# Two decoder layers on one core: the layer loop written out, page numbers read before the wait, and a new order of units in the down projections

## The reference, cut to what matters

```python
def swiglu(x, wg, wu, wd):
    return (jax.nn.silu(x @ wg) * (x @ wu)) @ wd        # D_MODEL 1024, D_FF 2816

def trunk_layer(h, ...):
    h = h + 0.5 * swiglu(rmsnorm(h, norm_ffn1), ffn1_gate, ffn1_up, ffn1_down)
    x = rmsnorm(h, norm_mix)
    z = x @ w_in + b_in            # split into the four mixers' columns and four gates
    # conformer convolution, retention, gated linear attention, differential attention
    merged = einsum(branches, w_branch, sigmoid(gates))
    h = h + merged @ w_out
    h = h + 0.5 * swiglu(rmsnorm(h, norm_ffn2), ffn2_gate, ffn2_up, ffn2_down)
```

## Time and profile before

| what | value |
|---|---|
| median of three executions | 2910.8 us |
| the profiled execution, its own time | 2914.48 us |
| its span, first to last instruction | 2912.9 us |
| PE busy | 2866.3 us, 98% |
| DVE busy | 2040.4 us, 70% |
| ACT busy | 1230.1 us, 42% |
| POOL busy | 121.1 us, 4% |
| DMA | 321.00 MB, 110 GB/s |
| a page of keys, request to landing, median | 2.9 us |
| a page of values, the same | 3.2 us |

### The profile page before, as it was taken

How to read it: one execution, slowest core, us unless ns; L and a number is a source line. 1 busy time by engine, 2 the same in 40 slices (tenths; PEclk the granted TensorE clock), 3 DMA queues, 4 the chain that set the end, 5 groups by cost and what they waited for, 6 DMA issues and landing times.

```text
span 2912.9 us, 59977 instructions
## 1 busy us (share of the span) xinstructions
PE 2866.3 (98%) x21668; PEld 2743.9 (94%) x21668; DVE 2040.4 (70%) x3643; ACT 1230.1 (42%) x2192; POOL 121.1 (4%) x219
## 2 busy tenths in 40 slices
PE   8999999999999999999999999999999999999998
PEld 7999999988889999999999999998878899999998
DVE  8889434567657688886488893346666576888854
ACT  6446223435325254454254452243352343544632
POOL 0000001220000000000000000012100000000000
PEclk9999999999999999999999999999999999999999
DMA  4223225562324312223222222436423243122232
GB/s 143 91 86 105 99 82 181 172 198 77 109 70 157 137 61 88 99 87 112 77 74 87 101 103 93 138 126 206 159 72 109 86 161 121 61 101 86 101 102 91
DMA packets 102131, 321.00 MB, mean 110 GB/s; under 512 B 13503, under 2 KB 30063, under 8 KB 100272
## 3 DMA queue, kind: packets, MB, share of 16 engines
q1 hardware_dynamic: 89424, 277.03, 27.3%
q0 software_dynamic: 12512, 41.43, 4.4%
HBM read 290.62 MB, written 29.12 MB: 110 GB/s over the span
## 4 chain that ended last, share of the span: by engine, by line
PE 90%; DVE 4%; issue 3%; POOLq 1%; ACT 1%; DMA 0%; POOL 0%; DVEq 0%; SPq 0%; ACTq 0%
PE ps L1304 46%; PE ps L1333 34%; PE ps L1483 3%; PE ps L1316 2%; PE ps L1749 1%; PE ps L1545 1%; POOLq L615 1%; DVE Z L2321 1%; DVE w_lo L1875 1%; PE ps L1621 0%; POOL vpage L616 0%; PE ps L1595 0%; PE ps L1771 0%; PE ps L1645 0%; PE ps L1644 0%
## 5 line engine op out<-in xcount | busy, mean ns | idle before, releaser
L1875 DVE TENSOR_TENSOR w_lo<-w_raw,w_hi 128x1024 fp32r<-128x1024 f32 x240 | 292.5, 1223 | 369.1 <-ACT w_hi L727 366.1
L1333 PE MATMUL ps<-x_more,w_hi 128*128 128x296 f32 x2112 | 460.3, 299 | 2.1 <-DVE p_copy L2028 1.4
L1333 PE MATMUL ps<-x_hi,w_hi 128*128 128x296 f32 x1408 | 421.6, 299 | 3.4 <-DVE hT L2146 2.1
L1333 PE MATMUL ps<-x_hi,w_lo 128*128 128x296 f32 x1408 | 422.2, 300 | 0.0
L1333 PE MATMUL ps<-x_lo,w_hi 128*128 128x296 f32 x1408 | 422.1, 300 | 0.0
L727 ACT ACTIVATE w_hi<-w_raw 128x1024 fp32r<-128x1024 f32 x224 | 234.7, 1053 | 396.7 <-PE ps L1304 198.8
L1304 PE MATMUL ps<-x_hi,w_hi 128*128 128x296 f32 x1600 | 371.7, 314 | 1.8 <-ACT hT L1054 1.6
L1913 DVE TENSOR_TENSOR w_lo<-w_raw,w_hi 128x512 fp32r<-128x512 f32 x444 | 299.5, 689 | 96.6 <-ACT w_hi L775 96.3
L1333 PEld LDWEIGHTS ps<-x_more,w_hi 128*128 128x128 f32 x2112 | 351.2, 188 | 4.3 <-DVE p_copy L2028 2.4
L1304 PE MATMUL ps<-x_lo,w_hi 128*128 128x296 f32 x1600 | 350.3, 300 | 0.0
L1304 PE MATMUL ps<-x_hi,w_lo 128*128 128x296 f32 x1600 | 349.8, 300 | 0.0
(11 more groups left out here) (367 smaller groups left out, 5089.5 us busy)
## 6 DMA issues: line engine op xcount, KB each, us to landing
w_raw<-wstream SPq DMA_DIRECT2D x420, 512.0 KB, 3.5
kpage<-cache_k SPq DMA_DIRECT2D x128, 128.0 KB, 2.9
vpage<-cache_v POOLq DMA_DIRECT2D x128, 128.0 KB, 3.2
gate_rows<-hT SPq DMA_DIRECT2D x48, 296.0 KB, 2.5
d_sg<-gate_rows SPq DMA_DIRECT2D x16, 888.0 KB, 4.7
h_rows<-hT SPq DMA_DIRECT2D x2, 1480.0 KB, 6.2
hT<-h_rows SPq DMA_DIRECT2D x2, 1480.0 KB, 6.3
hT<-h_in SPq DMA_DIRECT2D x4, 592.0 KB, 8.1
```

The lines of the kernel that those rows point to most:

```text
L1333: mm = pe.matmul(ps[:, bank, 0:HALF], wp[:, k, :], xp, start=new and k == 0 and n == 0, stop=k == KH - 1 and n == 2, skip_group_check=True)
L1875: v.tensor_tensor(w_lo[:, slot, :, :], w_raw[:, slot, :, :], w_hi[:, slot, :, :].bitcast(F32), ALU.subtract).then_inc(weights_low, 1)
```

## The change

Five edits:

1. On all five engines `Fori(0, DEPTH)` becomes a Python loop: the instructions of both layers stand one after the other and l is a constant. The shorter loops inside stay.
2. POOL's `load_values` takes the page numbers from `page_numbers`, which reads all 16 of a pass into registers; for passes 1 to 3 this stands ahead of the wait on `sample_pv`.
3. In the down projections PE takes the units in the order DOWN_ORDER: tile 0's unit 0, tile 1's unit 0, tile 0's units 1 and 2, tile 1's units 1 and 2, then tiles 2 and 3 as before; the same for tiles 4 to 7. `units_multiplied` is counted so that it keeps to the order of the stream: nothing at tile 1's unit 0, two at tile 0's unit 2.
4. OUT_PAIRS becomes (1, 2, 0, 3): tiles 1 and 5 go to pair 2, tiles 2 and 6 to pair 0. The waits of `begin` and of S1 in the next feed-forward stage are exchanged to fit; tile 1 and tile 2 of the down projection wait for DVE's quarters that read the banks.
5. At the end of a feed-forward stage the orders of DVE and ACT change, as below.

```diff
-OUT_PAIRS = (1, 0, 2, 3)
+OUT_PAIRS = (1, 2, 0, 3)
+DOWN_ORDER = ((0, 0), (1, 0), (0, 1), (0, 2), (1, 1), (1, 2)) + tuple((j, u) for j in (2, 3) for u in range(3))
...
-            def load_values(l, p):
-                for b in (2 * p, 2 * p + 1):
-                    for pg in range(PAGES):
-                        page = pl.value_load(pages[0:1, b * PAGES + pg:b * PAGES + pg + 1], min_val=0, max_val=POOL - 1)
-                        pl.dma_start(vpage[:, b % 2, pg, :], cache_v[ds(l * POOL + page, 1)]...).then_inc(values_loaded[b % 2], 16)
+            def page_numbers(p):
+                return [pl.value_load(pages[0:1, n:n + 1], min_val=0, max_val=POOL - 1) for n in range(2 * p * PAGES, 2 * (p + 1) * PAGES)]
+            def load_values(l, numbers):
+                for n, page in enumerate(numbers):
+                    b2, pg = divmod(n, PAGES)
+                    pl.dma_start(vpage[:, b2, pg, :], cache_v[ds(l * POOL + page, 1)]...).then_inc(values_loaded[b2], 16)
...
+                numbers = page_numbers(1)
                 pl.wait_ge(sample_pv, 1)
-                load_values(l, 1)
+                load_values(l, numbers)
...
 # ACT, last pair (after out_unit(2))
-                tanh(N0 + KF - 1)
                 hidden_tiles(6, 8)
                 act.wait_ge(products_done, last + 7)
-                hidden_tiles(8, 12)
                 out_unit(3)
-                hidden_tiles(12, KF)
+                hidden_tiles(8, 10)
+                tanh(N0 + KF - 1)
+                hidden_tiles(10, KF)
...
-            with act.Fori(0, DEPTH) as l:        # the same on pe, v, pl and sp
+            for l in range(DEPTH):
...
 # PE
-                pe.wait_ge(residual_added, l * 24 + 8 + 10 if f else l * 24 + 2)
+                pe.wait_ge(residual_added, l * 24 + 8 + 11 if f else l * 24 + 3)
                 begin(N0, 0)
...
+                    for j, u in DOWN_ORDER:
+                        pos = j * 3 + u
+                        unit_ready(l * QUADS + first // RING + i * 3 + pos // RING, pos % RING)
+                        if u == 0:
+                            pe.wait_ge(residual_added, l * 24 + r0 + i * 4 + j + 1)
+                        if (j, u) == (1, 0):
+                            pe.wait_ge(pair_steps, PAIR_STEPS * (hidden + KF - 1 + 2) + 3)
+                        elif (j, u) == (2, 0):
+                            pe.wait_ge(pair_steps, PAIR_STEPS * (hidden + KF - 1 + 2) + 6)
...
+                        if (j, u) == (0, 2):
+                            last.then_inc(units_multiplied, 2)
+                        elif (j, u) != (1, 0):
+                            last.then_inc(units_multiplied, 1)
...
 # DVE, last pair but one: hidden_low(0, 1) now stands ahead of its last low(W_A22)
 # DVE, last pair
-                hidden_low(0, 1)
                 split_low(quad0 + KF // 2, 0)
                 quarter(N, 0, tmp[:, 0, HALF:T], BANK_E, a_copy)
-                hidden_low(1, 2)
                 quarter(N, 1, c22, 1, e_copy)
-                hidden_low(2, 3)
+                hidden_low(1, 3)
                 quarter(N, 2, tmp[:, 0, 0:HALF], BANK_B, first_copy[1])
+                hidden_low(3, 6)
+                split_low(quad0 + KF // 2, 1)
+                hidden_low(6, 8)
+                split_low(quad0 + KF // 2, 2)
+                split_low(quad0 + KF // 2, 3)
                 gate_ready(N, 1)
-                split_low(quad0 + KF // 2, 1)
+                hidden_low(8, 10)
                 hidden_tile(N, 1, KF - 1, 7)
-                hidden_low(3, 10)
-                split_low(quad0 + KF // 2, 2)
                 hidden_low(10, KF)
-                split_low(quad0 + KF // 2, 3)
```

More of the change, by code:

```diff
@@ L610, in _ @@
         def _(pl):
-            def load_values(l, p):
-                for b in (2 * p, 2 * p + 1):
-                    for pg in range(PAGES):
-                        page = pl.value_load(pages[0:1, b * PAGES + pg:b * PAGES + pg + 1], min_val=0, max_val=POOL - 1)
-                        pl.dma_start(vpage[:, b % 2, pg, :], cache_v[ds(l * POOL + page, 1)].rearrange("a p n -> (a p) n")).then_inc(values_loaded[b % 2], 16)
+            def page_numbers(p):
[3 more added lines that the diff above has]
+                    b2, pg = divmod(n, PAGES)
+                    pl.dma_start(vpage[:, b2, pg, :], cache_v[ds(l * POOL + page, 1)].rearrange("a p n -> (a p) n")).then_inc(values_loaded[b2], 16)
             pl.dma_start(prm[:, :], params[0][:, 0:NP_ - P]).then_inc(params_loaded, 16)
@@ L632, in _ @@
             pl.sem_inc(mixers_open, 1)
-            with pl.Fori(0, DEPTH) as l:
+            for l in range(DEPTH):
                 pl.wait_ge(mixers_open, l + 1)
@@ L669, in _ @@
                 for p in (2, 3):
+                    numbers = page_numbers(p)
                     pl.wait_ge(sample_pv, p)
-                    load_values(l, p)
+                    load_values(l, numbers)
                 pl.wait_ge(sample_scores, 4)
@@ L1276, in _ @@
             act.activation(split_cols(ssum), pair(1), ACT.Copy).then_inc(squares_summed, SQUARED_FIRST)
-            with act.Fori(0, DEPTH) as l:
+            for l in range(DEPTH):
+                chain[0] = 0
                 ffn(l, 0, U_FFN1)
@@ L1416, in ffn, with down @@
                 pe.sem_inc(units_multiplied, 2 * KF)
-            def residual(l, r0, first, blocks, xh, xl, hidden):
-                units = len(blocks)
+            def down(l, r0, first, hidden):
                 with pe.Fori(0, 2) as i:
[L1421 to L1435, removed]
@@ new lines, in down @@
+                    for j, u in DOWN_ORDER:
[7 more added lines that the diff above has]
+                            pe.wait_ge(pair_steps, PAIR_STEPS * (hidden + KF - 1 + 2) + 6)
+                        bank, count = OUT_PAIRS[j], DOWN_BLOCKS[u]
+                        if j == 0:
+                            for k in range(count):
+                                pe.wait_ge(hidden_ready, hidden + 8 * u + k + 1)
+                                last = products(bank, pos % RING, (k, k + 1), 8 * u + k, hid_hi, hid_lo, start=u == 0 and k == 0,
+                                                stop=u == 2 and k == count - 1)
+                        else:
+                            last = products(bank, pos % RING, (0, count), 8 * u, hid_hi, hid_lo, start=u == 0, stop=u == 2)
+                        if (j, u) == (0, 2):
+                            last.then_inc(units_multiplied, 2)
+                        elif (j, u) != (1, 0):
+                            last.then_inc(units_multiplied, 1)
@@ L1854, in _ @@
             pe.wait_ge(bias_row_made, 2)
-            with pe.Fori(0, DEPTH) as l:
+            for l in range(DEPTH):
+                gate_blocks[0] = 0
                 ffn(l, 0, U_FFN1)
-                residual(l, 0, U_DOWN1, DOWN_BLOCKS, hid_hi, hid_lo, l * 2 * KF)
+                down(l, 0, U_DOWN1, l * 2 * KF)
                 project(l)
@@ L1866, in _ @@
                 ffn(l, 1, U_FFN2)
-                residual(l, 16, U_DOWN2, DOWN_BLOCKS, hid_hi, hid_lo, l * 2 * KF + KF)
+                down(l, 16, U_DOWN2, l * 2 * KF + KF)
         @block.vector
@@ L2074, in pair_ @@
                     low(N + 1, W_A12, g, w_sum)
+                    if kind == "one to go":
+                        hidden_low(0, 1)
                     low(N + 1, W_A22, g, w_sum)
@@ L2711, in _ @@
             v.wait_ge(bias_row_stored, 16)
-            with v.Fori(0, DEPTH) as l:
+            for l in range(DEPTH):
+                chain[0] = 0
                 ffn(l, 0, U_FFN1)
```

7 lines of the change are left out of this document (3 added, 4 removed).

## The result

The changed kernel takes 2891.2 us (median of 5 runs, 2888.8 to 2894.0) where the kernel before took 2909.9 us on the same chip (5 runs, 2905.7 to 2912.9). The ratio is 0.9936, interval 0.9925 to 0.9947: 18.6 us, 0.64%. On two other chips the same pair gave 2892.0 for 2911.4 (0.9938) and 2892.2 for 2911.4 (0.9930). The forecast was 2889.5 us, range 2883 to 2900.

The account below looks back on a forecast made before the run. PE, busy for 98% of the span, was taken to bound the kernel. Terms 7.1 + 9.3 + 3.4 + 1.5 = 21.3 us off 2914.5 gave 2893.2 profiled, 2889.5 us as median; own range 2885 to 2895, with A, B and D 2883 to 2900.

Parts of the forecast that it names:

- Down entries: Start of the four down projections: both PE stops go, 4 x 1.77 = 7.1 us; 5.9 if 0.3 us is lost at each.
- The replay of DVE's queue: Down entry, old durations in the new order: unit 0's low part starts at 275.45, units 2 and 3 end at 284.9 and 286.05.
- Rival B: Down entry: new wait for unit 3's low part, wanted 0.4 us after ready; 2.5 to 4.5 us lost, 2893 us; chance 0.09.
- Rival C: Down projections: late release of slots 1 and 3 runs the ring dry, 8 x 4.1 = 33 us, 2922 us; chance 0.04.
- Values: Sample attention, pass 2: wait for values and lowered clock go, 9.3 us for both layers, bounds 4.6 and 10.
- only keeps those 9.6 us: POOL, pass 2: no idle time of its own, so it keeps pass 1's 9.6 us; last request about 585 for 594.66.
- rival A: Sample attention: values stay late or the next wait takes half to all of 9.3 us; 2894 to 2899 us; chance 0.12.
- The keys of pass 3: Sample attention, next possible late data: last request at 599.6, landing some 2.9 us later, wanted at 603.6, margin 1.1 us.
- Start of layer 1: PE's 2.09 us pause is the loop's branch; without it 3.4 us gained, not 3.9; bounds 0 and 4.
- Registers in the mixers: Mixers, both layers: constants for registers save small operations before waits, 1.5 us, bounds 0 and 4.
- From the profiled execution to the median: Whole run: the profiled execution was 3.7 us above the median of 2910.8, so 2893.2 became 2889.5 us.
- Rival D: Layer 1's gap is data and DVE's order removes only the first down-entry stop: 12 us gained, 2899 us; chance 0.04.

Follow-up runs that it names:

- pages_only: The kernel before with edit 2 alone, page numbers read into registers ahead of the wait: 2902.8 us beside 2911.6, ratio 0.9967.
- layers_but_pe: The kernel before with the layer loop written out on every engine but TensorE: 2909.5 us beside 2911.4, ratio 0.9994.
- after_third: The changed kernel unchanged, run again as its third profiled execution: 2892.2 us beside 2911.4 for the kernel before, ratio 0.993.

## Why the prediction was right

*Down entries*, 7.1 us forecast, 8.0 measured, 2.0 at each entry: 1.8 by the first matmuls of the down projection, as forecast, and 0.2 more within its first tile, which I had not counted. The replay of DVE's queue was right to 0.1 us, and what it named as next late (unit 3's low part, ready 286.1, wanted 286.5) cost nothing: no wait for w_lo in the L1311 products. Rival B fell with that. Rival C, a ring that runs dry, fell too: the down projection behind the entry is one unbroken piece, 143.69 us.

*Values*, 9.3 us forecast, 8.6 measured in the profiled execution (7.6 to 9.3 over three). The cause was right, but one step failed, "only keeps those 9.6 us", and its size was off by half. The whole stage already lies 2.0 us sooner through the down entry, so that has to come off first. The last request of pass 2 went out at 587.85 for 594.66, 6.8 us sooner, of which 4.8 us are edit 2's, hardly more than the worst case of 4.6 us.

The other half was lost on POOL's queue. Pass 1 ended 6.4 us sooner by the same count (557.6 for 566.0), mainly because of the pause behind its 14th request. And POOL's stores don't follow at their own pace: in all 13 traces the first convs_out goes out 0.40 us after the last page requested before it has landed, and the second 0.33 us after the first has landed (wherever the trace has that landing). The last page of pass 1 took 4.6 us to land for 3.0 before. The last page of pass 2 took 5.2 us for 3.0, so of the 4.8 us only 2.5 reached PE, against a wait of 3.07 us: that is the 0.55 us left.

That the forecast of the gain held all the same is in part luck, since nearly all of the wait and the clock behind it come back as soon as 3 us are gained, and the forecast had 9.6 to spend. `pages_only` kept 6.1 us of the 9.6, and PE waited for no value. So a small part of rival A came true, a rest of 0 to 1.6 us in layer 0. The keys of pass 3, for which the prediction reckoned a margin of 1.1 us, were late in no execution (they landed 3.7 and 1.7 us ahead in two of the changed kernel, 0.4 us ahead in `pages_only`). The keys that came late, in `pages_only` and four of the later kernels, were those of pass 2.

*Start of layer 1*, 3.4 us forecast, 3.9 measured, inside the bounds of 0 to 4. I had said not 3.9, since DVE's chain to the product at 1478.06 would hold 0.5 us of it. It didn't: with the branches gone that product came at 1466.15 with the same 0.60 us wait in front as before (0.64). The reading of the 2.09 us as the branch was right against the row's releaser, hT: TensorE's branch record of 3.83 us covers the pause, and with the branch gone so is the pause.

*Registers in the mixers*, 1.5 us forecast. No run shows this term: what the mixers win or lose are steps of 1.5 us that the same kernel has from one execution to the next, and these would also hide it. The three others came to 20.5 us for the 19.8 forecast. The median ended 1.7 us above the forecast; that this is about the size of the term is no evidence.

*From the profiled execution to the median.* I subtracted 3.7 us for the kernel before. That fits the clock: the execution had the mean clock 0.993, near the lower end of the 0.992 to 0.998 that the runs show. The forecast gain of 21.3 us stands between the 23.3 us of the profiled pair and the 18.6 to 19.3 us of the medians; the medians are the fairer measure, and by them the gain was put 2.0 to 2.7 us too high.

Rival D is out by its own test: the gap at layer 1 was not data, and the new orders took both stops.

## What to carry to other kernels

When an engine's queue is late at a hand-over, replay it entry by entry with the old durations; here that named the times to 0.1 us. A reordering on one engine has to be judged with the order of the engine that it feeds: half of this change, DVE's without PE's, costs time. And set stages, not spans, against each other: two profiled executions of the same program differ by up to 5.5 us, most of it through the clock.

## What the runs showed that I had not expected

*The clock sets the spread of the runs.* Over the 17 runs of the kernel before on the last chip the time goes from 2905.2 us at a mean granted clock of 0.998 to 2918.4 us at 0.992: about 2.2 us for each 0.001. The changed kernel has the same: 2888.8 at 0.997, 2894.0 at 0.995. In the traces, what differs between executions of one kernel is mostly how long TensorE ran at 1.2 GHz instead of 2.4 in the mixers, where it stops for a moment again and again. What decides it from one execution to the next stays open.

*The same pause doesn't always cost clock.* Behind 2.09 us at the start of layer 1 the clock fell, behind 1.77, 1.72 and 1.57 us in three other kernels it did not. Of ten waits of 2.6 to 4.1 us for the values, in the five kernels with the old page loop, nine were followed by a lowered clock and one (2.57 us, `layers_but_pe`, layer 1) was not, which is most of its -1.5 us there.

*A taken branch of the long loop.* It cost ACT 2.6 us, DVE 2.9, POOL 3.6, SP 3.9 and TensorE 3.9 (in the trace of before, from the branch to the next operation of the same sequencer), and the short loops inside, taken many times, 0.15 to 0.35 us each. POOL stood as long, 3.7 us, where it left the loop, so its 3.6 can't be put down to the way back alone. The Trainium skill has the rule for this ("Runtime: NRT & Kernel Launch", "Instruction fetch mechanics"): only a target outside the pages that are held must be fetched. The trace agrees in that only the long loop's branches are slow; the fetch itself is in no row. All of it together is worth 2.7 us of 2910 here.

*POOL stops behind a burst of requests.* With the numbers in registers it puts out a request every 0.58 us, but after the 14th of pass 1 it stood for 2.91 us (before 556.43 above), and at the same place in the seven other profiled executions with this loop for 1.4 to 4.4 us. At the old pace of 1.15 us no such pause was there. No run was made for this, but the landing times in the traces point to what it waits for. In all eight executions and both layers the 15th request of pass 1 goes out 0.40 us after the 8th page of that pass has landed. It is that page and no other. In `after_third` the 13th page landed 0.2 us ahead of the 8th, and the 15th request still waited for the 8th, which took 8.2 us (window 549.4 to 549.8 us; count, size, us from request to landing):

```profile
vpage<-cache_v POOLq DMA_DIRECT2D x1, 128.0 KB, 8.2
```

At the old pace the 8th page of pass 1 had landed 3.5 us or more before the 15th request. So in these traces a faster pace of requests helps only as long as the page seven places back lands in time; what sets that distance stays open.
